# Transposing the next expert's tokens inside gate and up, and half-height warm-up products, in a hybrid encoder layer with 16 experts

## What is computed

```python
x = x + jnp.concatenate([o_att, o_conv], axis=-1) @ w_out[i]
h = rmsnorm(x, norm_ffn[i])
# hierarchical MoE: top-1 group, then top-2 experts in it
for e in range(N_EXPERTS):
    gu = t @ w_gate_up[e]                                   # 1024 -> 2 x 256
    y = (jax.nn.silu(gu[:, :D_EXPERT]) * gu[:, D_EXPERT:]) @ w_down[e]   # 256 -> 1024
    out = out + combine[:, e:e + 1] * y
```

## Time and profile before

| | |
|---|---|
| median of the runs | 603.12 us |
| profiled execution: time | 603.42 us |
| profiled execution: span, first to last instruction | 601.6 us |
| TensorE busy | 593.8 us, 99% |
| TensorE weight loads | 490.6 us, 82% |
| VectorE busy | 417.6 us, 69% |
| ScalarE busy | 330.3 us, 55% |
| granted TensorE clock, mean | 1.000 |

### The profile page before, as it was taken

How to read it: one execution, slowest core, us unless ns; L and a number is a source line. 1 busy time by engine, 2 the same in 40 slices (tenths; PEclk the granted TensorE clock), 3 DMA queues, 4 the chain that set the end, 5 groups by cost and what they waited for, 6 DMA issues and landing times.

```text
span 601.6 us, 8723 instructions
## 1 busy us (share of the span) xinstructions
PE 593.8 (99%) x3160; PEld 490.6 (82%) x3160; DVE 417.6 (69%) x773; ACT 330.3 (55%) x595; POOL 68.1 (11%) x109
## 2 busy tenths in 40 slices
PE   8999999999999999999999999999999999999997
PEld 6888989888887777888887887778888888878886
DVE  5426962344542666746877789899999999788863
ACT  7752200322232675656555566799999998961211
POOL 0060000000000000100100114142121220210000
PEclk9999999999999999999999999999999999999999
DMA  8916655120312412212314778989999999785611
GB/s 333 404 34 229 236 220 205 36 95 10 102 38 71 183 36 106 87 54 106 106 72 154 248 246 296 405 316 414 411 410 411 412 412 376 290 314 198 227 42 64
DMA packets 39042, 126.52 MB, mean 210 GB/s; under 512 B 6448, under 2 KB 7472, under 8 KB 38968
## 3 DMA queue, kind: packets, MB, share of 16 engines
q1 hardware_dynamic: 33224, 112.97, 50.4%
q0 software_dynamic: 4896, 12.59, 5.4%
q10 hardware_dynamic: 880, 0.41, 0.2%
HBM read 113.33 MB, written 23.10 MB: 227 GB/s over the span
## 4 chain that ended last, share of the span: by engine, by line
PE 93%; DMA 2%; DVE 2%; ACT 1%; issue 1%; SPq 0%; DVEq 0%; POOLq 0%; POOL 0%; ACTq 0%
PE bank L509 21%; PE bank L511 20%; PE bank L510 20%; PE bank L1958 7%; PE bank L540 6%; PE bank L541 6%; PE bank L539 5%; PE bank L1975 3%; PE bank L1994 3%; PE bank L2109 2%; PE bank L2268 1%; DMA moe_rows<-moe_y,slot_row 1%; DMA pick<-moe_rows 1%; DMA colv<-in_cols 1%; DVE w_split L1733 0%
## 5 line engine op out<-in xcount | busy, mean ns | idle before, releaser
L504 DVE TENSOR_TENSOR w_split<-w_raw,w_split 128x1024 fp32r<-128x1024 f32 x33 | 40.5, 1228 | 22.5 <-ACT w_split L499 22.3
L509 PE MATMUL bank<-w_split,moe_xT 128*128 128x512 f32 x120 | 48.4, 404 | 0.8 <-DVE w_split L1733 0.8
L1023 ACT ACTIVATE sq_tmp<-bank 128x512 f32<-128x512 f32 x12 | 7.2, 599 | 75.5 <-PE bank L511 75.5
L511 PE MATMUL bank<-w_split,moe_xT 128*128 128x512 f32 x120 | 47.0, 391 | 0.0
L510 PE MATMUL bank<-w_split,moe_xT 128*128 128x512 f32 x120 | 46.8, 390 | 0.0
L499 ACT ACTIVATE w_split<-w_raw 128x1024 fp32r<-128x1024 f32 x33 | 34.7, 1054 | 18.9 <-PE bank L541 16.6
L988 ACT ACTIVATE s<-s,mn 128x512 f32<-128x512 f32 (+1 forms) x48 | 30.9, 645 | 18.7 <-DVE mn L1441 18.7
L488 DVE TENSOR_TENSOR w_split<-w_raw_more,w_split 128x1024 fp32r<-128x1024 f32 x32 | 37.9, 1216 | 2.7 <-ACT w_split L482 2.2
L509 PE MATMUL bank<-w_split,x3T 128*128 128x512 f32 (+1 forms) x104 | 39.5, 379 | 0.2 <-DVE x3T L1907 0.2
L511 PE MATMUL bank<-w_split,x3T 128*128 128x512 f32 (+1 forms) x104 | 38.8, 373 | 0.0
L510 PE MATMUL bank<-w_split,x3T 128*128 128x512 f32 (+1 forms) x104 | 38.8, 373 | 0.0
(11 more groups left out here) (329 smaller groups left out, 1592.1 us busy)
## 6 DMA issues: line engine op xcount, KB each, us to landing
w_raw<-in_w_moe SPq DMA_DIRECT2D x32, 512.0 KB, 5.5
w_raw_room<-in_w_moe SPq DMA_DIRECT2D x30, 512.0 KB
w_raw_more<-in_w_moe SPq DMA_DIRECT2D x30, 512.0 KB
w_raw<-in_w_in SPq DMA_DIRECT2D x23, 512.0 KB
pick<-moe_rows SPq DMA_DIRECT2D x12, 512.0 KB, 4.8
bias_rows<-bias_table SPq DMA_DIRECT2D x1, 4096.0 KB
w_raw<-in_w_out SPq DMA_DIRECT2D x8, 512.0 KB
toep<-bias_rows SPq DMA_DIRECT2D x4, 896.0 KB, 7.1
```

What stands on the lines that cost most here:

```text
L504: nc.vector.tensor_tensor(W[:, u % WS, 1], raw(u)[0], f(W[:, u % WS, 0]), ALU.subtract).then_inc(lo_done, 1)
L509: nc.tensor.matmul(out, hi, whi, start=first, stop=False)
L511: return nc.tensor.matmul(out, hi, wlo, start=False, stop=last)
```

## The change

On TensorE alone two places change. The eight transposes of x(t+1) move from behind unit 3 of gate and up to directly behind the transposed activations, between units 1 and 2, for t from 2 to 14. Of the ten warm-up products the last two go, and six others take their place: float32r products of 64 rows by 192 columns, alternately on the lower and the upper half of the rows. Their outputs go to banks 6 and 7, which nothing reads then.

```diff
             pe.wait_ge(dch, 2)
-            for _ in range(10):
+            for _ in range(8):
                 pe.matmul(bank[7][:], warm[:, 0:P], warm[:, P:5 * P], start=True, stop=True)
+            rows_of = warm[:].bitcast(F32R)
+            for _ in range(3):
+                for m in range(2):
+                    r = slice(m * HD, (m + 1) * HD)
+                    pe.matmul(bank[6 + m][:, 0:192], rows_of[r, 0:P], rows_of[r, P:320], start=True, stop=True)
             w = W[:, 0]
...
                 else:
                     pe.wait_ge(lp_dxt, n * 2 + 2)
                     turn_x(2)
-                gate_up(t, range(2, 4))
                 if 1 < t < LAST:
                     turn_x(t + 1)
+                gate_up(t, range(2, 4))
                 if t > 1:
                     down(t - 1)
```

## The result

The changed kernel takes 612.96 us, median of six runs (612.32 to 613.19), against 603.11 (602.56 to 603.61) for the kernel before: ratio 1.0166, 95% interval 1.0155 to 1.0177. It is slower by 9.85 us. The forecast was 604.8 us with a range up to 606.2: the sign was right, the size was wrong by nearly a factor of six.

A forecast was written before the change was run, and what follows sets the result against it. It took TensorE, busy 593.8 of 601.6 us, to bound the kernel. Span 601.6 + 1.7 (late x) - 0.1 (transposes) + 0.1 (warm-up) = 603.3; on the median of 603.12 this gave 604.8 us, range 602.9 to 606.2.

The forecast's parts named there:

- What bounds the kernel: Whole kernel: TensorE bounds it, busy for 593.8 of 601.6 us, with no gap in the steady expert's 9.32 us.
- the ring: Experts' loop of TensorE's unit 2, ACT's unit 4, DVE, x, TensorE: each late x costs 0.14 us, 12 times, 1.7 us.
- I cost this at nothing: POOL's indirect load of x(t+1), needed 2.73 us earlier, still comes in time, issued over 18 us ahead: no loss.
- The transposes themselves: TensorE's ten transposes in a row per expert: 0.01 us saved for each of 13 experts, 0.1 us in all.
- The warm-up: Kernel start: six small products replacing two full ones delay line 539's start at 6.84 by 0 to 0.34 us, taken 0.1.
- rival B: Kernel start: smaller warm-up products don't hold the clock up, real ones begin at the lower level; +2.1 us, 606.9; chance 0.05.
- Nothing gives the time back: Behind the experts: all waits for the last outputs, so time lost in the experts is not regained.
- A: Experts: x's lateness is absorbed by the hidden weight load, at most 0.1 us each; within 0.2%, 603.4 us; chance 0.30.
- C: Experts: DVE fills up, its 0.67 us shift adds in full; period 9.99, 8 us lost, 611; chance 0.05.
- D: Experts' transposes become cheaper by 0.1 us each, of 1.10; faster by over 1.2 us; chance 0.05.

The follow-up runs named there:

- e5: Kernel before, with x's transposes between units 2 and 3 and the load of x issued one place earlier in POOL's queue: 602.68 us, ratio 0.9994.
- e6: Kernel before plus the moved transposes, the earlier load of x, and unit 4 put behind x(t+1) in ACT's and DVE's order: 603.43 us, ratio 1.0006.
- e3: Changed kernel with the indirect load of x one place earlier in POOL's queue, ahead of an output's store: 604.84 us, ratio 1.0033.
- e1: Kernel before with only the warm-up part of the change: 603.09 us, ratio 0.9999.
- e2: Kernel before with only the move of the transposes: 612.21 us, ratio 1.015.
- e4: Kernel before with only the load of x issued one place earlier in POOL's queue: 602.94 us, ratio 1.0.
- e7: Kernel before with only x's transposes moved between units 2 and 3, the load left late: 605.2 us, ratio 1.0035.
- e8: Kernel before with the move alone, load left late, and half the weight bytes of experts 5 to 15 loaded: 607.33 us, ratio 1.0067.
- e9: Kernel before with eight full warm-up products and no small ones: 603.85 us, ratio 1.0011.
- e10: Kernel before with eighteen full warm-up products instead of ten: 604.06 us, ratio 1.0018.

## Why the prediction was wrong

**What bounds the kernel, and the ring: right.** The move does what the prediction followed step by step. In the changed kernel, in an expert of which x came late (ACT, DVE, then TensorE):

```profile
444.75 1.06 ACT L482 ACTIVATE w_split<-w_raw 128x1024 fp32r<-128x1024 f32 x1 [1.69 <-PE bank L511]
...
445.84 1.23 DVE L488 TENSOR_TENSOR w_split<-w_raw,w_split 128x1024 fp32r<-128x1024 f32 x1 [1.27 <-ACT w_split L482]
...
447.32 1.28 DVE L1773 TENSOR_TENSOR moe_xT<-bank,moe_xT 128x512 fp32r<-128x512 f32 x2
...
448.65 0.50 PE L509 MATMUL bank<-w_split,moe_xT 128*128 128x512 f32 x1
448.99 0.40 PE L510 MATMUL bank<-w_split,moe_xT 128*128 128x512 f32 x1
```

Unit 4 waits for unit 2's use, DVE waits for unit 4, x ends at 447.32 + 1.28 = 448.60, the product starts 0.05 us later and the second one 0.34 behind it, as in the earlier trace rows. e5 and e6 cut the ring at two different places and both give the period back. The term was a little small: 0.18 us for each expert instead of 0.14, 2.2 in place of 1.7 us. In e3, from a late load at 435.67, unit 2's last product starts 5.11 us behind it (440.78; predicted 5.08), ACT 0.49 and DVE another 1.09 behind that, x is done 2.76 later (predicted 2.74), and the next load starts 0.05 behind it. So the missing 0.04 us is 0.03 in TensorE's own pace and 0.02 in DVE's stretch, less 0.01 between ACT and DVE.

**The step that failed: "I cost this at nothing".** The prediction took the load at 448.59 as being for the expert three ahead and concluded that there were over two periods, 18 us. The index was right and the distance wrong. POOL runs behind TensorE: in its step t the load of x(t+3) stands behind the store of expert t-1's output, and that output comes when TensorE is already in expert t+1. x(t+3) is transposed within expert t+2. So from the issue at 448.59 to the use at 459.20 there were 10.6 us:

```profile
459.20 1.04 PE L1958 MATMUL bank<-cst,moe_x 128*128 128x128 f32 x8
```

The load itself takes 8.3 to 9.6 in the changed kernel, and the change asked for 2.73 of the 1.0 to 2.3 that this left. Counting the transposes in the trace instead of the index in the source would have shown it. How long this transfer takes the trace of before doesn't tell, since nothing waits for it, but the earlier trace rows gave a sign (DMA share 1.03) that I used only for the weights. That no wait for a load was seen says that it was in time, not by how much.

The loss by this term is not 12 times the shortfall of 1.7 us. Without lateness there are 7.9 us from issue to use (423.11 to where x would have been used, 430.98). A late x delays the use of the next one as well, but not its load, which is issued behind an earlier store: the load at 412.25 had 9.24 us, until 421.49, and came in time. So an expert with a wait is often followed by one without, and eight late loads make 7.4 us.

**The transposes themselves.** The value of 0.01 us for each expert was low; e6 shows 0.03 to 0.04, just inside the bound of 0.04.

**The warm-up.** In the profiled execution of the changed kernel line 539 starts at 7.20 us instead of 6.84, a loss of 0.36 against an upper bound of 0.34 and a taken 0.1. But that difference can't be put down to the edit. With the edit the start is at 7.20, 7.06 (e3) and 6.96 (e1); with the ten products as before it is at 6.84 to 6.90 (before, e2, e4, e5, e7), and at 7.08 (e8) and 7.10 (e6). Where the clock rises differs from execution to execution, whatever the warm-up. The starts of the changed kernel (the first two lines are real products), of e6 (ten products) and of e1:

```profile
5.81 0.79 PE L2033 MATMUL bank<-h_T_prompt,w_split 128*128 128x512 f32 x1
6.40 0.63 PE L2035 MATMUL bank<-h_T_prompt,w_split 128*128 128x512 f32 x1
...
7.20 0.40 PE L539 MATMUL bank<-h_T_prompt,w_split 128*128 128x512 f32 x1
```
```profile
6.12 0.63 PE L2035 MATMUL bank<-h_T_prompt,w_split 128*128 128x512 f32 x1
...
7.10 0.45 PE L539 MATMUL bank<-h_T_prompt,w_split 128*128 128x512 f32 x1
```
```profile
4.32 0.38 PE L2025 MATMUL bank<-warm_ops 128*128 128x512 f16 x1
4.63 0.58 PE L2030 MATMUL bank<-warm_ops 64*128 64x192 f32 x6
5.63 0.50 PE L2033 MATMUL bank<-h_T_prompt,w_split 128*128 128x512 f32 x1 [0.42 <-ACT w_split L956]
```

In the changed kernel the two real products are modelled at 0.6 to 0.8 us each, the six small ones end at about 5.9, and line 539 follows late. In e1 the last full warm-up product already takes 0.38, and TensorE is idle for 0.42 us before the first real one. In the median of e1 the edit doesn't show (1.0 within 0.1%). The low chance of rival B rested on the small products counting; e9 speaks for that, and there, with eight full ones alone, the low pace lasted some 3 to 4 us longer in the traced execution.

**"Nothing gives the time back": not so, and why is open.** In the two profiled executions 1.08 us came back behind the experts. TensorE waits there 0.5 us for DVE's first full pick in the kernel before, and not at all in the changed one. That stretch, from the transposes of expert 14's activations to the end, takes 88.2 to 88.8 us in the five traces without this wait and 88.9 to 89.5 in the seven with it. But lateness alone doesn't decide it: e7 comes out of the experts 2.2 us later than the kernel before and waits 0.9 us, while e1 comes out only 0.15 later and doesn't wait. The three that come out over 4 us later (after, e2, e8) all don't wait, so a late arrival may play a part; no run separates it from the scatter. The prediction had no such term, and without this gain the miss would have been 1.1 us larger. Where the missing 0.6 us of e10's delay went stays open for the same reason.

**Rivals.** A fell with e3, where the ring alone costs 1.8 us. C fell: DVE is busy 8.85 us of a period of 9.49. B and D did not occur. The case that came true, a transfer that is late because its use was moved forward, was not among the rivals, though the first part of the prediction names the transfer.

No version here beats the kernel before beyond its interval: e5 (0.9994) and e4 (1.0) stand level with it.

## What to carry to other kernels

When a step is moved forward, the margin of each thing that it reads has to be measured as a distance in the trace, from the issue that fetched it to this very use, with the time under way subtracted; a loop index in another engine's queue tells nothing about that distance. A missing wait is no margin. And where one queue issues both stores and loads, a load that follows a store is as late as the engine that produces the store: putting it ahead was a small edit here and was worth 8 us in the changed kernel, though nothing in the kernel before, where the load was in time by an estimated 1 us or more.

## What the runs showed of the hardware

An indirect load of 128 rows of 4 KB, issued 1.3 us behind an indirect store of the same size, took 8.3 to 9.6 us from issue to landing, with the DMA engines at 1.02 to 1.03 of their time (383 to 416 GB/s) but for the last two of these loads, whose own share was 0.86 and 0.90; 7.2 to 7.8 us with the engines as full but no store just ahead of it (e4); and 3.8 to 6.9 us behind a store with half of the weights' bytes (e8; 254 GB/s and 0.78 between 422.7 and 440 us).

The clock of TensorE reads 1.00 in the profile's windows throughout, also in stretches where products of 512 columns start 0.427 us apart (1.2 GHz) and not 0.227 (2.4 GHz). In the first microseconds the distance of starts is the better witness. By it the clock rose at about 5.7 us in the kernel before, near 6.8 in the changed kernel, before 4.4 in e1, and at 10.6 in e9. With the warm-up of ten products unchanged it rose at about 4.5 us in one trace (e8) and near 6.9 in another (e6). The Trainium skill ("TensorE: Matmul & The Clock Gate", What's actually happening) says that the transition point varies from run to run; these traces agree, with 2.4 us between the earliest and the latest under an unchanged warm-up. The latest of them went with a pause of 0.61 us between the warm-up and the first real product, but e8 had one of 0.59 us with the clock already up and kept it, so no run here shows that the pause was the cause.
